# First attention of a two-block kernel: transposes placed singly between passes of scores and of V

## The reference

```python
p_cmp = masked_softmax(einsum(q, k_cmp), cmp_end <= t)   # 31 compressed keys
o_cmp = p_cmp @ v_cmp
p_sel = masked_softmax(einsum(q, k_g), pos <= t)         # selected blocks: all 8 of them here
o_sel = p_sel @ v_g
p_win = masked_softmax(einsum(q, k_w), window of 512)    # causal, the whole sequence
o_win = p_win @ v_w
o = g[0] * o_cmp + g[1] * o_sel + g[2] * o_win           # sigmoid gates
return o @ w_out
```

## Time and profile before

| what | value |
|---|---|
| median of 3 runs | 1956.4 us (1956.35 to 1958.35) |
| the profiled execution, its own time | 1956.99 us |
| its span, first to last instruction | 1955.3 us |
| busy: TensorE / loads / VectorE / ScalarE / GpSimd | 1847.5 / 1505.4 / 943.7 / 776.1 / 896.9 us |
| mean granted TensorE clock | 0.980 of full speed |
| first attention | about 166 to 327 us of the span |

### The profile page before, as it was taken

One profiled execution on the slowest core, in us unless ns is written; L12 is line 12 of the kernel. 1 busy time (PEld: TensorE's weight loads), 2 busy tenths in 40 slices (PEclk: granted clock), 3 DMA queues, 4 the chain that ended last, 5 costly groups with the idle time before them and its releaser, 6 DMA issues.

```text
span 1955.3 us, 24484 instructions
## 1 busy us (share of the span) xinstructions
PE 1847.5 (94%) x8842; PEld 1505.4 (77%) x8842; DVE 943.7 (48%) x1309; ACT 776.1 (40%) x1368; POOL 896.9 (46%) x643
## 2 busy tenths in 40 slices
PE   5899999999899999999999879998899999999996
PEld 4787878888788888888677448887688888888875
DVE  7235997502468814875821561237665320022435
ACT  5446887433333222224433332357323442233232
POOL 3144777563244444444434044449645344444441
PEclk9999999999999999999999889999999999999997
DMA  4331001342022233234212003220132223222221
GB/s 152 118 108 44 1 2 44 108 151 86 22 89 105 100 114 111 104 109 149 87 65 86 22 1 108 86 87 1 56 106 87 93 101 107 87 90 103 101 71 44
DMA packets 24122, 161.45 MB, mean 83 GB/s; under 512 B 2928, under 2 KB 3440, under 8 KB 5104
## 3 DMA queue, kind: packets, MB, share of 16 engines
q1 hardware_dynamic: 23040, 158.35, 23.1%
q10 hardware_dynamic: 1008, 2.12, 0.3%
HBM read 158.36 MB, written 2.10 MB: 82 GB/s over the span
## 4 chain that ended last, share of the span: by engine, by line
PE 85%; DVE 6%; POOL 4%; ACT 3%; issue 2%; DMA 1%; DVEq 0%; SPq 0%; ACTq 0%; POOLq 0%
PE psum L534 82%; PE psum L836 2%; POOL q_st L2480 1%; POOL tmp L2480 1%; DVE tmp L1812 1%; ACT w_hi_r L1136 1%; DVE sqt L2180 1%; DVE acc L2188 1%; DMA ring<-in_panels 1%; POOL big_r L2495 0%; DVE tmp L1810 0%; DVE q_st L1803 0%; DVE h_lo L1984 0%; DVE big L2372 0%; DVE tmp L2362 0%
## 5 line engine op out<-in xcount | busy, mean ns | idle before, releaser
L2411 POOL TENSOR_TENSOR w_lo<-ring,w_hi_r 128x1024 fp32r<-128x1024 f32 (+3 forms) x280 | 665.7, 2398 | 844.1 <-ACT w_hi_r L1136 844.1
L534 PE MATMUL psum<-h_hi,w_hi_r 128*128 128x512 f32 x1200 | 473.6, 395 | 19.5 <-DVE h_lo L1732 8.1
L534 PE MATMUL psum<-big_r,w_hi_r 128*128 128x512 f32 (+1 forms) x1568 | 467.6, 381 | 7.3 <-DVE xt L1771 1.9
L534 PE MATMUL psum<-h_lo,w_hi_r 128*128 128x512 f32 x1200 | 470.4, 392 | 0.0
L534 PE MATMUL psum<-h_hi,w_lo 128*128 128x512 f32 x1200 | 470.3, 392 | 0.0
L1136 ACT CAST w_hi_r<-ring 128x1024 fp32r<-128x1024 f32 x288 | 285.7, 1041 | 367.1 <-PE psum L534 360.8
L534 PEld LDWEIGHTS psum<-big_r,w_hi_r 128*128 128x128 f32 x1568 | 289.8, 188 | 65.4 <-issue 6.1
L534 PE MATMUL psum<-big_r,w_lo 128*128 128x512 f32 (+1 forms) x784 | 298.3, 380 | 0.0
L534 PEld LDWEIGHTS psum<-h_hi,w_hi_r 128*128 128x128 f32 x1200 | 227.6, 190 | 73.8 <-issue 22.6
L534 PEld LDWEIGHTS psum<-h_hi,w_lo 128*128 128x128 f32 x1200 | 227.3, 189 | 47.9
L534 PEld LDWEIGHTS psum<-h_lo,w_hi_r 128*128 128x128 f32 x1200 | 227.4, 190 | 47.2 <-issue 0.5
(11 more groups left out here) (340 smaller groups left out, 2526.2 us busy)
## 6 DMA issues: line engine op xcount, KB each, us to landing
ring<-in_panels SPq DMA_DIRECT2D x147, 1024.0 KB, 4.8
xt<-in_x SPq DMA_DIRECT2D x4, 512.0 KB, 6.3
out<-big SPq DMA_DIRECT2D x8, 256.0 KB, 2.1
big<-in_mem ACTq DMA_DIRECT2D x1, 1024.0 KB, 4.7
q_st<-in_ple ACTq DMA_DIRECT2D x1, 512.0 KB, 3.4
spare<-in_w_gate ACTq DMA_DIRECT2D x1, 192.0 KB, 6.2
spare<-in_w_k ACTq DMA_DIRECT2D x1, 128.0 KB, 8.9
params<-in_params ACTq DMA_DIRECT2D x1, 114.0 KB, 4.6
```

The source lines that it names most:

```text
L534: return nc.tensor.matmul(o, l, r, start=start, stop=stop, **kw)
L2411: g.tensor_tensor(w_lo[:, p], ring[:, p], plain(w_hi[:, p]), ALU.subtract) \
```

## The change

`nsa_score`, `nsa_turn` and `nsa_product` become generators that yield after each pass or transpose (not after a mask). `nsa_long` runs the scores of part k+4 and then the products of step k; after each of its yields one transpose of part k is issued, and the transposes that are left over follow at the end. So a step reads pass, transpose, pass, transpose, mask, pass, transpose and so on. The waits of the transposes now come up after the first pass of the step. The signal `scores` comes behind the mask as before, `turned` on the last transpose, `summed` on the last product pass.

```diff
--- before.py
+++ after.py
@@ -813,11 +813,14 @@
                     if part["br"] == CMP:
                         mm(o, nsa_q(part["pair"], x, part["par"], raw=True)[:, cs], kcmp[:, g * NCMP:(g + 1) * NCMP],
                            True, False)
+                        yield
                         m = cmp_mask[:, qt * NCMP:(qt + 1) * NCMP]
                     else:
                         q = nsa_q(part["pair"], part["h0"] + x, part["par"])[:, cs]
                         mm(o, q, nsa_key(g, part["br"], 0)[:, 0:nk], True, False)
+                        yield
                         mm(o, q, nsa_key(g, part["br"], 1)[:, 0:nk], False, False)
+                        yield
                         m = causal[:, :]
                     n = m.shape[1]
                     last = mm(psum[:, b, (x + 1) * nk - n:(x + 1) * nk], ident_bf[:, :], m, False, True)
@@ -833,9 +836,11 @@
                     for k in range(0, nk, P):
                         n = min(P, nk - k)
                         c0 = (k // P * nh + x) * P
-                        last = nc.tensor.transpose(psum[0:n, 4 + w % 2, c0:c0 + P], p[:, x * nk + k:x * nk + k + n],
+                        done = nc.tensor.transpose(psum[0:n, 4 + w % 2, c0:c0 + P], p[:, x * nk + k:x * nk + k + n],
                                                    ident[:, :])
-                last.then_inc(ns["turned"], 1)
+                        if (x, k + P >= nk) == (nh - 1, True):
+                            done.then_inc(ns["turned"], 1)
+                        yield
 
             def nsa_product(n, kt):
                 x = sums[n]
@@ -845,23 +850,35 @@
                 if x["br"] == CMP:
                     pe.wait_ge(ns["lo"], x["end"] + 1)
                     last = mm(o, vcmp[:, x["g"] * P:(x["g"] + 1) * P], nsa_cmp[x["u"] % 2], False, False)
+                    if kt == x["blocks"] - 1:
+                        last.then_inc(ns["summed"], 1)
+                    yield
                 else:
                     if kt == 0:
                         pe.wait_ge(ns["lo"], x["end"] + 1)
                     v = nsa_value(kt, x["br"], x["g"])
                     cs = slice(kt * S, (kt + 1) * S)
                     mm(o, v, nsa_weights(0, x["br"])[:, cs], x["first"] and kt == 0, False)
+                    yield
                     last = mm(o, v, nsa_weights(1, x["br"])[:, cs], False, x["last"] and kt == x["blocks"] - 1)
-                if kt == x["blocks"] - 1:
-                    last.then_inc(ns["summed"], 1)
+                    if kt == x["blocks"] - 1:
+                        last.then_inc(ns["summed"], 1)
+                    yield
+
+            def nsa_long(k):
+
+
+                if 0 <= k + LEAD < NW:
+                    yield from nsa_score(parts[k + LEAD])
+                for n, kt in products_at.get(k, ()):
+                    yield from nsa_product(n, kt)
 
             for k in STEPS:
-                if 0 <= k + LEAD < NW:
-                    nsa_score(parts[k + LEAD])
-                if 0 <= k < NW:
-                    nsa_turn(parts[k])
-                for n, kt in products_at.get(k, ()):
-                    nsa_product(n, kt)
+                turns = nsa_turn(parts[k]) if 0 <= k < NW else iter(())
+                for _ in nsa_long(k):
+                    next(turns, None)
+                for _ in turns:
+                    pass
             pe.wait_ge(ns["probs"], NW)
 
             def nsa_rhs(k):
```

## The result

The changed kernel takes 1969.7 us (median of 4 runs, 1969.48 to 1969.87) against 1957.0 for the kernel before (4 runs, 1956.35 to 1958.35): 12.7 us or 0.65% slower, ratio 1.0064 with a 95% interval of 1.0046 to 1.0081. The forecast was 1971 in a range of 1961 to 1979.

The account below looks back on a forecast made before the run. TensorE's order was taken to set the time, with little room on the other engines. Issue time 7.3, waits 6.6 and step 0's 0.7 summed to +14.6 us, against the median of 1956.4 giving 1971 us, range 1961 to 1979.

Parts of the forecast that it names:

- A transpose behind a long pass: Some 250 transposes come to stand behind a long pass; taken at 0.11 us as in a row, no gain.
- Rival B: Transposes between long passes cost 0.06 us, loads hidden: -12.5, giving 1951.2 us without new waits; chance 0.06.
- Issue time: TensorE's instruction costs with new neighbours in the attention: +7.3 us, bounds +3.5 and +11.
- The term of the masks: 102 causal masks now stand behind a transpose, taken at 0.08 us each: +1.0 us (0 to 5).
- passes behind a mask: 67 more product passes and 4 more score passes stand behind a mask, 0.055 us more each: +3.9 us.
- Waits: Transposes' waits for VectorE's remainders move ahead of most score passes; 30 steps stay short: +6.6 us.
- step 0: First attention step reaches its wait for the scaled part 0 early: 0.6 to 0.8 us idle, +0.7.
- Steps 33 and 94: Transposes move ahead of their remainder: 0.55 us lost with nil slack, 0.72 lost with slack 0.37.
- its loop closes: Last transpose, copy, remainder, next transposes in a 512 step: 1.57 us available, 1.47 needed, if neither engine is otherwise occupied.
- Rival A: Issue time only, as other engines catch up: 1964.4 us; chance 0.17 with what lies between (1961 to 1966).
- Rival C: Later last transpose pushes copy and remainder behind VectorE's maximum and ScalarE's exponential: 1979 us; chance 0.17 (over 1975).
- D: No change: low issue bound 3.5 and waits absorbed, 1957 to 1960 us, or hidden loads with all waits; chance 0.08.

Follow-up runs that it names:

- e3: Kernel before, with copy and remainder of the transposed probabilities cut to 32 columns each (times only): 1954.2 us, ratio 0.9987.
- e4: Changed kernel with the same copy and remainder cut to 32 columns each (times only): 1964.0 us, ratio 1.0036.
- e5: Kernel before, but the last causal mask of a step's scores stands behind all four transposes: 1960.0 us, ratio 1.0018.
- e1: Changed kernel's interleaving only between passes of V; scores and first transpose as in the kernel before: 1962.1 us against 1957.6, ratio 1.0027.
- e2: Changed kernel's interleaving only between passes of scores; leftover transposes follow, then the passes of V in a run: 1966.6 us, ratio 1.0059.
- e6: Kernel before, but one transpose stands ahead of the last causal mask of a step's scores: 1957.8 us, ratio 1.0003.
- e8: Changed kernel with one more yield, so a transpose follows the last mask of a part's scores: 1971.2 us, ratio 1.0066.
- e7: e6, plus three transposes between high and low passes in the eight parts with 128-wide scores: 1957.4 us, ratio 0.9999 against the kernel before.

## Why the prediction was right, point by point

**The bound.** TensorE's order sets the time, and what it loses in the attention is lost in the total: +13.1 us from the first score pass to the first pass of the output product (161.6 to 174.7), +12.5 in the span. Of the 13.1, 1.1 lie ahead of the mask of part 14, 11.5 in the stretch and 0.4 behind part 103.

**A transpose behind a long pass.** Taken at 0.11, it is 0.11. Rival B, with loads that hide, is out. The Trainium skill's rule ("TensorE: Matmul & The Clock Gate", Part 2) that weight loads are pulled ahead agrees with this trace, in that the pass behind a transpose costs its plain 0.23. But the load was not what spaced the transposes: they cost the same 0.11 with a 512 pass around them.

**Issue time**, +7.3 forecast, bounds 3.5 and 11: about 4.4 to 5 measured (4.4 in the stretch from part 14, 4.5 to 5.0 by e3 and e4). Mechanism right, three terms mis-sized. A mask behind a transpose took 0.056 on the median of 102 and not 0.08: -2.4. A transpose in the compressed scores took 0.143 on the median of 58 and not 0.16: -1.0. A transpose behind a 128-wide pass took 0.13 on the median of 32, where the flat price said 0.11: +0.7. Together 7.3 - 2.7 = 4.6. The term of the masks, for which no row stood, was taken near the pass row, and lay below both ends: its bound of 0 was the right end, and the measured term (-1.4) lies below even that. The term of passes behind a mask was right: 0.289 on the median of 67 against 0.234, and e5 shows it alone.

**Waits**, +6.6 in 30 steps, and +0.7 in step 0. Measured in the part from 14 to 103: 10.0 us in 27 places where the kernel before has 2.8 in 11, so +7.2; over the whole attention 11.1 in 30 places where the kernel before has 4.8 in 15 (that forecast and trace both count 30 is chance: some places waited before). Steps 33 and 94, forecast to lose 0.55 and 0.72 more, lose 0.28 more (0.51 for 0.23) and 0.94 more: nearly right in sum, wrong one by one. "The slack is nil" overlooked that step 33 waited already. Step 0 idles for 0.76. The sign that was named for the waits, TensorE's idle time put down to h_lo growing to 8 us or more, did not come: that view has 3.3. It was the wrong scale, as it hides idle time under overlapping records; by end-to-end cost the waits grew as forecast. But the reading gave all of it to the front. By e1 some 2 us belong to the late last transpose, of which I had said that its loop closes with 0.1 to spare; e2 has 6.1 at the front. So the sum of the waits was right in part because two errors of some 1 to 2 us cancelled: the front somewhat less than forecast, the back not nothing.

**The sum.** +14.6 forecast, 12.7 measured; three differences make it. Issue time was 2.3 too high (about 5.0 in the whole attention for 7.3). Waits were some 1.8 too low: 7.2, with 0.7 more ahead of part 14, 0.4 behind part 103 and 0.8 in step 0, come to 9.1 for 7.3. The third is a term that the forecast didn't have, and it is luck: the lower clock near 170 us. It lasts 6.8 us in the profile of the kernel before, 5.9 of them once TensorE is busy again (170.87 to 176.8), and 3.4 in that of the changed kernel (172.2 to 175.6), so the changed kernel was spared an estimated 1.2 us, half of the difference of 2.5. Two of the two-microsecond windows of the kernel before show it (the granted clock is again the third number from the end); the mean of 0.98 in the earlier trace rows hides it.

```profile
170.00:172.00 2.00, 1.13 (x7) 1.13 (x8) 1.15 (x4) 1.83 (x6) 0.78 (x2) 0.50 0.00 0
...
176.00:178.00 2.00, 2.00 (x14) 1.32 (x13) 1.66 (x6) 1.75 (x5) 1.61 (x5) 0.80 0.00 0
```

At the same clock the attention would have grown by an estimated 14.3 us (13.1 + 1.2). Rival A (waits absorbed, 1964.4) is out by the 7 us of waits. Rival C is out in its size, but its mechanism is that of e1. B and D are out.

**What stays open.** Why a mask ends only 0.056 after a transpose and 0.072 after a pass: ends of matmuls are modelled in these records, so the two may share one true cost and the difference may belong to the transposes. e6 supports a real gain of 0.012 a step (-1.1 in 89 steps) and no more. Whether e8 is faster than the changed kernel in whole runs was not settled; its stretch is shorter. Each stretch stands in one profile of its kernel, so its scatter from execution to execution was not measured.

## What to carry to other kernels

Price a reordering by pairs: an instruction's cost is its end minus its predecessor's end, for the predecessor that it will have, and look at what comes to stand behind the small ones. When an instruction that carries a wait moves ahead, compare, step by step, how far it moves with the slack in the trace between the releasing event and its present start; what is short is lost, less what the longer steps give back. Mixing short and long instructions on TensorE hides nothing where the short ones cost the same with a long one around them as in a row (here 0.109 us either way). Before a difference of a microsecond or two is put down to a change, look at the granted clock of both profiles, window by window.

## What the runs showed of the hardware

- Float32 transposes of 128 columns cost 0.109 us each, in a row as well as behind passes of 256 to 512 columns, though one starts 0.07 after a mask does. That the load doesn't space them is read from this; that their own streaming does is an inference. They cost more behind a mask (0.116), behind a 128-wide pass (0.13) and behind a 31-wide one (0.143).
- A pass of 512 columns costs 0.289 behind a bf16 mask instead of 0.234 behind a transpose (0.287 in e5), and two passes behind a mask cost 0.51 in the kernel before. That a part of its load shows there is the likely reason; no run separates it.
- The lower clock near 170 to 180 us, behind idle stretches of TensorE of 1.0 and 1.88 us, lasts 3.4 us in the profiles of the changed kernel, e1, e3, e5, e6 and e7, and 6.8 in those of the kernel before, e2, e4 and e8. The profiles of e1 to e8 all have another one between 506 and 523 us, of 3.4 or 6.8, which those of the kernel before and the changed one don't have, in code that is the same. Each 3.4 us is worth an estimated 1.7, as much as some of the effects under study.
